# adaLN products beside gate/up: eight of eleven weight blocks summed over k on VectorE, then over the partitions by TensorE

## What is computed

```
def adaln_params(cvec, w, b):
    m = jax.nn.silu(cvec) @ w + b              # w: 1024 x 9216 in each layer
    return m.reshape(m.shape[:-1] + (N_MOD, D_MODEL))

def swiglu(u, wg, wu, wd):
    return (jax.nn.silu(u @ wg) * (u @ wu)) @ wd

def ffn_sublayer(x, shift, scale, gate, g_pre, g_post, wg, wu, wd):
    y = swiglu(modulate(x, g_pre, shift, scale), wg, wu, wd)
    return x + FFN_RES * gate * rms_norm(y, g_post)
```

## Time and profile before

| what | us |
|---|---|
| time before, median of 3 runs | 2112.97 |
| lowest and highest of them | 2108.23, 2122.46 |
| profiled execution, its own time | 2119.63 |
| span of the profiled execution | 2117.9 |
| TensorE busy in it | 1968.5 (93%) |
| VectorE busy in it | 903.6 (43%) |
| ScalarE busy in it | 761.5 (36%) |

### The profile page before, as it was taken

The page is one execution under the profiler, slowest core; times in us unless marked ns, Lnnn a source line. Parts: engine busy times, 40 slices in busy tenths (PEclk is TensorE's granted clock), DMA queues, the critical chain, the costliest instruction groups (busy, mean ns, idle before and its releaser), DMA issues. The chain is left out here.

```text
span 2117.9 us, 25112 instructions
## 1 busy us (share of the span) xinstructions
PE 1968.5 (93%) x10421; PEld 1542.6 (73%) x10421; DVE 903.6 (43%) x1283; ACT 761.5 (36%) x1107; POOL 240.0 (11%) x325
## 2 busy tenths in 40 slices
PE   5899999999898886999999989999999899979997
PEld 2677777865786673777777857888788388759997
DVE  1432232245646644433232254333222765855544
ACT  3422221226436532422222234222222555645443
POOL 3011110001731000011110000000000242100000
PEclk7899999988898878899999988999999899989998
DMA  8355553343322024455543343333233433155653
GB/s 282 99 179 172 166 171 121 95 125 80 80 51 65 16 61 121 138 163 176 178 149 120 96 145 88 100 97 91 77 95 104 118 91 89 39 161 142 186 156 115
DMA packets 366178, 254.01 MB, mean 120 GB/s; under 512 B 30579, under 2 KB 343245, under 8 KB 366065
## 3 DMA queue, kind: packets, MB, share of 16 engines
q1 hardware_dynamic: 345360, 182.97, 31.5%
q0 software_dynamic: 20704, 69.44, 10.0%
HBM read 251.30 MB, written 1.07 MB: 119 GB/s over the span
## 5 line engine op out<-in xcount | busy, mean ns | idle before, releaser
L316 PE MATMUL bank<-u_hi,w_hi 128*128 128x512 f32 (+2 forms) x1872 | 693.7, 371 | 14.1 <-DVE u_lo L972 6.8
L317 PE MATMUL bank<-u_lo,w_hi 128*128 128x512 f32 (+2 forms) x1872 | 682.8, 365 | 0.0
L318 PE MATMUL bank<-u_hi,w_lo 128*128 128x512 f32 (+2 forms) x1872 | 682.4, 365 | 0.0
L300 DVE TENSOR_TENSOR w_lo<-raw,w_hi 128x2048 fp32r<-128x2048 f32 (+2 forms) x182 | 373.8, 2054 | 331.7 <-ACT w_hi L292 331.6
L316 PEld LDWEIGHTS bank<-u_hi,w_hi 128*128 128x128 f32 (+1 forms) x1872 | 357.7, 191 | 114.7 <-issue 57.5
L318 PEld LDWEIGHTS bank<-u_hi,w_lo 128*128 128x128 f32 (+1 forms) x1872 | 357.2, 191 | 57.5 <-issue 1.1
L317 PEld LDWEIGHTS bank<-u_lo,w_hi 128*128 128x128 f32 (+1 forms) x1872 | 357.9, 191 | 53.6 <-issue 0.9
L292 ACT ACTIVATE w_hi<-raw 128x2048 fp32r<-128x2048 f32 (+2 forms) x182 | 311.4, 1711 | 165.2 <-PE bank L318 149.2
L316 PE MATMUL bank<-ht_hi,w_hi 128*128 128x512 f32 (+1 forms) x704 | 257.2, 365 | 9.5 <-DVE ht_lo L999 8.2
L317 PE MATMUL bank<-ht_lo,w_hi 128*128 128x512 f32 (+1 forms) x704 | 256.6, 365 | 0.0
L318 PE MATMUL bank<-ht_hi,w_lo 128*128 128x512 f32 (+1 forms) x704 | 256.4, 364 | 0.0
(11 more groups left out here) (233 smaller groups left out, 1515.3 us busy)
## 6 DMA issues: line engine op xcount, KB each, us to landing
ada_slot<-in_ada_w_dram POOLq DMA_DIRECT2D x128, 512.0 KB, 4.5
raw<-in_ffn_wg_dram SPq DMA_DIRECT2D x88, 512.0 KB, 4.0
raw<-in_ffn_wu_dram SPq DMA_DIRECT2D x88, 512.0 KB, 5.3
raw<-in_ffn_wd_dram SPq DMA_DIRECT2D x64, 384.0 KB, 3.6
raw<-in_ffn_wd_dram SPq DMA_DIRECT2D x64, 320.0 KB, 4.1
raw<-in_w_in_dram SPq DMA_DIRECT2D x32, 512.0 KB, 4.7
ada_first<-in_ada_w_dram SPq DMA_DIRECT2D x4, 2048.0 KB, 21.0
raw<-in_w_in_dram SPq DMA_DIRECT2D x16, 256.0 KB, 4.6
```

What stands on the lines that cost most here:

```text
L300: nc.vector.tensor_tensor(w_lo[s][:, 0:size], raw[s][:, 0:size], w_hi[s][:, 0:size].bitcast(F32), ALU.subtract).then_inc(lo_ready[s], 1)
L316: nc.tensor.matmul(acc, wh, xh, start=first, stop=False)
L317: nc.tensor.matmul(acc, wh, xl, start=False, stop=False)
L318: return nc.tensor.matmul(acc, wl, xh, start=False, stop=last)
```

## The change

In each of the two gate/ups with blocks beside them, the first eight of the eleven blocks are no longer multiplied by TensorE. VectorE multiplies each k tile of a quarter (128x512) by the silu of `c` of its rows, once for the latent vector and once for the context vector (e = 0, 1), and adds over the eight k tiles: four instructions a quarter, sixteen a block. The sums of a block are two tiles of 128x512; the sums over the partitions are still to be made. TensorE makes them for two blocks at a time, with four matmuls against a column of ones in a window of zeros (`add_pick`), into bank 4. The last three blocks of the eleven stay on TensorE as they were. The quarter with even number is summed after `ht_lo` of the unit, the odd one after the `w_lo` that follows. The slots of `ada_slot` are freed by VectorE then, and rows are taken out of the bank and turned one i later.

More of the change, by code:

```diff
@@ L175, in hybrid_block_kernel @@
         ht_hi, ht_lo = overlay(HT_AT, HT_SIZE, [("ht_hi", [P, FT, TOK], F32R), ("ht_lo", [P, FT, TOK], F32R)])
+        sums_a = overlay(HT_AT + SUM_TILE * TOK * 4, 4 * BLOCK * 4, [(f"ada_sum{n}", [P, BLOCK], F32) for n in range(4)])
+        sums_b = overlay(HT_AT + (FT + SUM_TILE) * TOK * 4, 4 * BLOCK * 4, [(f"ada_sum{n}", [P, BLOCK], F32) for n in range(4, 8)])
+        ada_sum = [*sums_a, *sums_b]
         (Y_ffn,) = overlay(U_AT, U_SIZE, [("Y_ffn", [P, KT, TOK], F32)])
@@ L246, in hybrid_block_kernel @@
         first_loaded = [sem(f"first_loaded{g}") for g in range(FIRST_BLOCKS)]
+        ada_part, ada_added = sem("ada_part"), sem("ada_added")
         ada_summed, ada_rows, ada_turned, mod_part, mod_done, pick_ready, tables = (
```

## The result

| | median us | runs |
|---|---|---|
| before | 2116.74 (2106.81 to 2123.42) | 19 |
| changed | 2106.22 (2101.36 to 2120.88) | 19 |

The ratio of the changed kernel to the one before is 0.9954, with a 95% interval of 0.9941 to 0.9968: 7 to 12 us faster, where 30 were forecast. The effect is real and a third of its forecast size; the time lies outside the range. The kernel before has a higher median here than in the three runs that the forecast started from (2116.74 against 2112.97 us). A second set of runs gave a ratio of 0.9939 (0.9908 to 0.9970).

What follows compares the result with a forecast made beforehand. TensorE was taken to bound the gate/ups with blocks: 39.7 - 9.4 - 0.2 = 30.1 us off the median of 2112.97 gives 2082.9, say 2083 us. The range was 2070 to 2094, reaching 2103 with two rivals.

Steps and rivals of the forecast that it cites:

- added wait: VectorE waits for each quarter's landing in gate/up: slot cycle 8.3 to 8.9 us against 10.88, so no stop.
- What bounds the kernel: In gate/up with blocks beside it, TensorE is always busy and sets the time; two quarters cost 1.24 us a unit.
- What goes from TensorE: Eight blocks' quarters in each of two gate/ups leave TensorE, 1.24 us a unit: 39.7 us, all on the path.
- What comes to TensorE: `add_partitions` four times in each gate/up adds 9.4 us to TensorE; lone turns add 0.2 us.
- Does VectorE hide its part?: Sums at 0.75 us an instruction make VectorE's round in gate/up 10.4 us, under 10.88, ready half a us early.
- the first rival: VectorE becomes the bound in the gate/ups if its instructions take 0.9 us or more: about 2097 us, chance 0.09.
- The clock: Granted clock stays 0.95 in gate/up; the fall after its end, worth 1.7 us, stays; a few us left each way.
- Late quarters: Quarters queue behind `raw` transfers in gate/up, landing in 9.8 us; VectorE waits every unit: 2164 us, chance 0.04.
- Smaller losses eat a third or more, 2095 to 2105: The clock or smaller losses, at no named place, take a third or more of the gain: chance 0.06.
- The lock-out: GpSimd is kept from issuing quarter loads while VectorE works in gate/up, round 13.5 us: 2162 us, chance 0.02.

Runs made afterwards that it cites:

- Experiment 7: Changed kernel with one more VectorE instruction of 128x512 in each summed quarter: 2108.72 us, ratio 0.9952 to the kernel before.
- experiment 8: Changed kernel with two more VectorE instructions of 128x512 in each summed quarter: 2119.76 us, ratio 1.0010 to the kernel before.
- experiment 1: Changed kernel, TensorE taking quarter 1 of the first block left on it in the middle of unit 17: 2093.82 us, ratio 0.9888 to the kernel before.
- experiment 2: Changed kernel, VectorE summing the last quarter of the last summed block ahead of `w_lo`: 2094.13 us, ratio 0.9892 to the kernel before.
- experiment 3: Changed kernel with four instead of eight blocks of each gate/up summed on VectorE: 2126.03 us, ratio 1.0021 to the kernel before.
- experiment 5: Changed kernel, last summed quarter ahead of `w_lo`, last `add_partitions` between quarters 0 and 1 of TensorE's first block: 2095.30 us, ratio 0.9892 to the kernel before.

## Why the prediction was wrong

The forecast was 2083 us and the measured median is 2106.2, 23 us more. Of these, 14.0 us are a stop that the sum didn't have, 3.8 the base (2112.97 instead of 2116.74), 2.1 the sizes of TensorE's own terms, and about 3 stay open. The mechanism of the gain was right; the term "added wait" was put at nothing, and that is what failed.

- **What bounds the kernel.** Right. TensorE sets the time of these stages, and the price of a break could be read from the beat.
- **What goes from TensorE.** Right in kind, 2.5 us too high. Unit 1 of the very first gate/up gained nothing: its interval is 12.28 us after and 12.28 in both traces of before, as it starts when its `w_lo` is ready (TensorE waits 1.67 us for it after the change, 0.65 and 0.77 before) and not when TensorE is free. 31 units at 1.20 us make 37.2 us instead of 39.7.
- **What comes to TensorE.** Right: 12.08 - 10.88 = 1.20 us for a lone `add_partitions`, 12.96 - 12.08 = 0.88 for the one in company (I took 1.0), 0.1 more for each lone turn (11.83 - 10.88 = 0.95 against 0.83). Together 9.2 against 9.6.
- **Does VectorE hide its part?** Yes. One sum takes 746 ns, as L1357 said, and VectorE had 1.3 to 1.8 us to spare before the next product, more than the half I worked out. Four follow each other in 2.73 us, 0.66 from start to start, and not in 3.0. The rows held that number: the 0.87 us for two instructions of 256 columns run to the end of the second, which takes 0.48 itself, so they start 0.39 apart, and 0.39 + 0.27 = 0.66; I had divided 0.87 by two. Experiment 7 used most of that room up at no price in the beat, experiment 8 went past it and paid. So VectorE does become the bound, as the first rival said, from about 1.6 us more work a unit than the change brought (an estimate: the mean of 1.29 and 1.83 us to spare), between the 1.2 of experiment 7 and the 2.4 of experiment 8.
- **The added wait: the step that failed.** "As a cycle of one slot: 3.0 + 0.1 + 0.72 + 4.5 to 5.1 = 8.3 to 8.9 us against 10.88. No stop" holds where VectorE frees a slot and VectorE takes the next load out of it. I worked out that cycle only, and it holds: VectorE never waits for a quarter in the trace. At the handover the one who frees is VectorE, late in the unit, and the one who takes is TensorE, which wants both quarters at the unit's end. By my own numbers: the odd slot is freed at 11.0 after the silu and filled by 16.9, and TensorE asks at 10.9 plus one quarter. That is a stop of about 5 us twice, and it stood in numbers that I had. Measured: 3.93 and 3.65 us, shorter because VectorE ran faster and freed the slot at 10.2 (259.16 - 248.95). Experiments 1 to 3 confirm it: the stop goes when TensorE asks later, shrinks when VectorE frees earlier, and moves with the handover.
- **The clock.** I wrote that falls stay as they are. This stop brings one of its own in each gate/up; with the second break of 1.0 us it makes 3.9 and 3.7 us of waiting into 6.6 and 7.4.
- **Rivals.** "Late quarters" named the right kind of wait and put it on the wrong engine, in every unit instead of once. "Smaller losses eat a third or more, 2095 to 2105" was nearest to the time, without a mechanism. The lock-out didn't happen: GpSimd issued at 108.07 in 0.72 us while VectorE stood in a stretch without gaps. What the Trainium skill, "SBUF — State Buffer", section "Who interferes with whom", says in its narrow form (VectorE instructions with two SBUF inputs hold up GpSimd's reads of SBUF, and not its writes) agrees with this, if an issue only writes to SBUF, which no run here shows; that `tensor_scalar` holds up an issue can't be seen here, since none falls onto one.

The sum with what was measured: 37.2 - 9.2 = 28.0 us off, 14.0 back at the handover: 14.0 gained. The gate/ups say the same, 510.97 us in the second trace of before and 496.87 in the first of the changed kernel, 14.1 less. The runs say 10.5 (7 to 12). The remaining 2 to 7 us lie outside the gate/ups with blocks, and I can't place them; by the ratio of the second set, 13 us gained, it is only 1. The rest of the span varies between 1598.0 and 1615.1 us over ten traces of all kernels, without order by kernel (1607.5 and 1598.0 for the changed one, 1605.5 and 1609.1 for the one before). The scatter goes in good part with the granted clock. Of the changed kernel's 19 runs the shortest (a span of 2099.6 us) had a mean clock of 0.954 and the longest (2119.1) one of 0.943. Over the 107 runs whose mean clock is known, a clock lower by 0.001 goes with about 1.4 us more within a kernel (an estimate, from a straight line through them). By this the ten runs of experiment 3, with a mean of 0.949 where the kernel before had 0.953, would lose about 5 us, some 2 of them by their own stops; that covers a part of its excess. For the changed kernel (0.950) it is about 4 us, but some 3 of them are its own stops (10 us at the lower level in the first trace, 0.0024 of the mean), which the 14.0 already hold. So most of the 2 to 7 us isn't explained by it, and it stays open whether the change slows the other stages a little.

Of all versions, experiments 1, 2 and 5 are the fastest, 1.1% under the kernel before and 0.6% under the changed one, and can't be told apart.

## What to carry to other kernels

When work on a stream of buffers moves from one engine to another, check the slot cycle not only for the steady state but at each place where the consumer changes: who frees the slot, how late in its round, and when does the *next* consumer ask? With two slots there is one load of slack, and a consumer that takes two at once spends it. Both cures cost nothing in buffers: let the new consumer take the second item half a round later, or let the old one free its last slot before its other work.

## What was not expected of the hardware

- The long stretches of gate/up don't follow the granted clock between 0.95 and 1.00. One trace, the first of before, was granted 0.95 there and the nine others 1.00, and 48 matmuls take 10.88 us in all ten. Only the breaks differ: 1.24 us for two quarters at 0.95, 1.20 at 1.00.
- All twelve waits of 2.6 to 4.5 us for a quarter inside a gate/up were followed by some microseconds at the lower level (a mean of 0.63 and 0.80 in the two stretches above, 0.50 in the second gate/up from 1037 to 1043 us); those of 0.57 and 0.36 us in experiment 2 were not. But such a wait doesn't always bring a fall: at the end of layer 1's first gate/up TensorE waits 2.80 us in each of the ten traces, and the 8 us after it have a mean clock of 1.00 in three of them and 0.61 to 0.82 in seven. What decides it isn't shown. It is one way in which executions of the same program come to differ.
- The price of a stop in the changed kernel, with the second break, was 1.7 and 2.0 times the wait that stands in its row (6.56 for 3.93, 7.42 for 3.65).
- Small matmuls that share a break can pack better or worse by their order alone: with `add_partitions` between two quarters unit 17 took 13.4 us, where as many, as one `add_partitions` ahead of two quarters, take 12.96.
